# The convolution-gate product in three passes on split operands, in place of plain float32

## The reference, cut to what matters

```
for l in range(2):
    h = rms_norm(x, norm_g[l]) * (1.0 + scale) + shift
    z = h @ w_in[l]
    q_lat, kv_lat, k_rope, mla_gate, conv_in, conv_gate = split(z)
    q, kv = rms_norm(q_lat) @ w_q_up[l], rms_norm(kv_lat) @ w_kv_up[l]
    mla_out = attention(q, k, v) * silu(mla_gate)
    u = u_val * sigmoid(u_gate)                      # from conv_in
    u = causal_depthwise_conv(u, dw_w[l], dw_b[l])   # 31 taps
    u = silu(layer_norm(u)) @ w_pw[l] + b_pw[l]
    conv_out = u * silu(conv_gate)
    x = x + gate * (concat([mla_out, conv_out]) @ w_out[l])
```

## Time and profile before

| | |
|---|---|
| timed runs | 2514.95, 2525.88, 2526.59 us; median 2525.88 |
| the profiled execution | 2515.07 us, its span 2513.3 us |
| TensorE busy (matmuls) | 2300.4 us, 92% |
| VectorE busy | 1775.0 us, 71% |
| ScalarE busy | 909.1 us, 36% |
| `cgate`, layer 0 | from 351.29 us on |
| last mean matmul, layers 0 and 1 | 428.27 and 925.88 us |

### The profile page before, as it was taken

How to read it: one execution, slowest core, us unless ns; L and a number is a source line. 1 busy time by engine, 2 the same in 40 slices (tenths; PEclk the granted TensorE clock), 3 DMA queues, 4 the chain that set the end, 5 groups by cost and what they waited for, 6 DMA issues and landing times.

```text
span 2513.3 us, 41861 instructions
## 1 busy us (share of the span) xinstructions
PE 2300.4 (92%) x16517; PEld 2193.2 (87%) x16517; DVE 1775.0 (71%) x2368; ACT 909.1 (36%) x1330; POOL 48.8 (2%) x61
## 2 busy tenths in 40 slices
PE   2189999999899998998988999988999999999998
PEld 2189998789899977898988998778999999999997
DVE  6777898795778987959768583578866666554443
ACT  1054322324434123244443441135544444443333
POOL 0000000000000000005000000000000000000000
PEclk9698999999889999998999998989999999999999
DMA  8869754787687547967968793346865555556552
GB/s 300 313 227 345 259 169 142 260 304 232 208 303 262 167 158 234 314 222 234 343 217 293 258 333 114 101 151 202 275 210 183 184 182 181 180 169 182 181 182 95
DMA packets 413233, 557.40 MB, mean 222 GB/s; under 512 B 25139, under 2 KB 362103, under 8 KB 412868
## 3 DMA queue, kind: packets, MB, share of 16 engines
q1 hardware_dynamic: 409536, 550.70, 66.9%
q0 software_dynamic: 1120, 2.18, 0.5%
q10 hardware_dynamic: 2468, 3.07, 0.3%
HBM read 553.72 MB, written 2.17 MB: 221 GB/s over the span
## 4 chain that ended last, share of the span: by engine, by line
PE 78%; DVE 12%; DMA 5%; ACT 3%; issue 2%; SPq 0%; DVEq 0%; ACTq 0%
PE gemm L1354 71%; DVE ada_acc L921 4%; DMA ada_raw<-in_ada_w 4%; PE stat L1374 2%; PE stat L1381 1%; DVE w_lo L948 1%; DVE scr L976 1%; DVE h_lo L981 1%; ACT w_hi L675 1%; DMA ada_raw<-in_w_ada 1%; DVE ss L1119 1%; ACT h_full L711 0%; PE bankS L1500 0%; PE bankS L1499 0%; DVE q_tok L1126 0%
## 5 line engine op out<-in xcount | busy, mean ns | idle before, releaser
L948 DVE TENSOR_TENSOR w_lo<-w_raw,w_hi 128x1024 fp32r<-128x1024 f32 (+1 forms) x564 | 671.3, 1201 | 431.6 <-ACT w_hi L675 429.4
L1354 PE MATMUL gemm<-h_hi,w_hi 128*128 128x256 f32 x3136 | 900.5, 287 | 47.4 <-DVE h_lo L981 19.9
L1354 PE MATMUL gemm<-h_lo,w_hi 128*128 128x256 f32 x3136 | 895.9, 286 | 0.0
L1354 PE MATMUL gemm<-h_hi,w_lo 128*128 128x256 f32 x3136 | 895.6, 286 | 0.0
L675 ACT ACTIVATE w_hi<-w_raw 128x1024 fp32r<-128x1024 f32 (+1 forms) x564 | 571.6, 1028 | 740.8 <-PE gemm L1354 590.2
L1354 PEld LDWEIGHTS gemm<-h_hi,w_hi 128*128 128x128 f32 x3136 | 611.6, 195 | 50.7 <-issue 34.6
L1354 PEld LDWEIGHTS gemm<-h_lo,w_hi 128*128 128x128 f32 x3136 | 611.4, 195 | 0.2
L1354 PEld LDWEIGHTS gemm<-h_hi,w_lo 128*128 128x128 f32 x3136 | 610.7, 195 | 0.0
L921 DVE SCALAR_TENSOR_TENSOR ada_acc<-ada_raw,c_act,ada_acc 128x1024 f32<-128x1024 f32 x360 | 460.9, 1297 | 34.7 <-DMA ada_raw<-in_ada_w 28.7
L1354 PE MATMUL gemm<-G_hi,w_hi 128*128 128x256 f32 x704 | 199.3, 283 | 3.1 <-DVE w_lo L948 3.1
L1354 PE MATMUL gemm<-G_lo,w_hi 128*128 128x256 f32 x704 | 199.2, 283 | 0.0
(11 more groups left out here) (269 smaller groups left out, 2562.7 us busy)
## 6 DMA issues: line engine op xcount, KB each, us to landing
w_raw<-in_w_in SPq DMA_DIRECT2D x264, 512.0 KB, 5.5
ada_raw<-in_ada_w SPq DMA_DIRECT2D x192, 512.0 KB, 5.3
w_raw<-in_w_up SPq DMA_DIRECT2D x176, 512.0 KB, 3.5
ada_raw<-in_w_ada SPq DMA_DIRECT2D x168, 512.0 KB, 5.2
w_raw<-in_w_out SPq DMA_DIRECT2D x96, 512.0 KB, 5.4
w_raw<-in_w_down SPq DMA_DIRECT2D x64, 512.0 KB, 3.9
ada_late<-in_w_ada SPq DMA_DIRECT2D x24, 512.0 KB, 4.5
w_raw<-in_w_down SPq DMA_DIRECT2D x32, 384.0 KB, 3.6
```

What stands on the lines that cost most here:

```text
L948: dve.tensor_tensor(w_lo[:, fixed % PARTS, 0:sz], w_raw[:, fixed % RAW, 0:sz], w_hi[:, fixed % PARTS, 0:sz].bitcast(F32), ALU.subtract).th ...
L1354: last = pe.matmul(half(g, k, q), left, right, start=(kt == 0 and j == 0), stop=(u == len(g.units) - 1 and t == nk - 1 and j == len(parts) ...
```

## The change

`cgate` becomes a split product on `h_hi` and `h_lo`, like `gate` before it, and `h_full`, its copies and its semaphore go. The order of the products, the loads and the convolution's steps stay as written.

```diff
-        h_full = at("h_full", W2 + 8, [P, KT, T])
...
-        h_full_ready = sem("h_full_ready")
...
-            G["cgate", l] = product("cgate", wi, 4, CB, full, 4, "a", h_full, None, plain(O_CG))
+            G["cgate", l] = product("cgate", wi, 4, CB, full, 4, "a", h_hi, h_lo, plain(O_CG))
...
-                    if r < LAYERS:
-                        for t in range(KT):
-                            ins = act.activation(h_full[:, t, :], buf[:, t, :], ACT.Identity, bias=mod[:, shift, t:t + 1])
-                        ins.then_inc(h_full_ready, 1)
...
-                pe.wait_ge(h_full_ready, l + 1)
```

## The result

The changed kernel takes 2537.47 us (median of 6 runs, 2534.11 to 2540.95), the kernel before on the same chip 2523.07 us (6 runs, 2514.95 to 2526.59). The ratio is 1.0061, with a 95% interval from 1.0047 to 1.0076: slower by 0.6%, where 1.0% was forecast (2552 us, range 2533 to 2565). Of the profiled executions the one after took 2534.11 us with a span of 2532.3 us, 19.0 us more than the span of before.

What follows compares the result with a forecast made beforehand. TensorE and VectorE were both full where `cgate` stands, TensorE ending last; the change would make VectorE pacemaker. 2 x 14.8 - 6.7 + 2 x 1.5 = +25.9 us on the median 2525.88 gave 2552 us, range 2533 to 2565.

Steps and rivals of the forecast that it cites:

- The case as computed: Whole kernel: VectorE paces `cgate`, start gaps close, some clock is lost; +25.9 us, 2552 us, own range 2541 to 2559, 74%.
- the rival in which half of the lateness is absorbed: VectorE's chain after the last mean: load waits or convolution layout give back some 8 us a layer; 2536 us, 10%.
- The two levels of execution: Timed runs of the kernel before: executions lie at two levels 11 us apart, the profiled one at the lower.
- VectorE becomes the pacemaker, pitch 5.86 us: Beside `cgate`'s units c0 to c15: a split plus 12 convolution operations takes 5.86 us against TensorE's 2.88; 14.8 us later a layer.
- The convolution ends at 441.5, TensorE still arrives last: End of the `cgate` stage: convolution done at 441.5, TensorE at 443.1, so TensorE is last by 1.6 us.
- Clock, +1.5 us a layer: TensorE's clock may fall between waits for splits; loss bounded by 0 and 3 us a layer, 1.5 taken.
- a rival: TensorE's clock stays down through `kv` and `q`, as in `krope`: 6.5 us a layer in place of 1.5, 2562 us, 12%.
- Twelve waits of some 3 us for `w_lo`: TensorE in `cgate`: waits of some 3 us before nearly every unit from c6 on, some 12 a layer.
- The third mean must wait, to 416.0, and is over before c15: In `cgate`: third mean waits for 2 operations behind c14's split, to 416.0, ending before c15, the last of 16 units.
- Both gaps go, -6.7 us: Start of each layer: without `h_full` copies TensorE's idle of 3.04 and 3.69 us goes, -6.7 us for two layers.
- Against which time: Base of the sum: +26 us added to the median before, 2525.88, giving 2552; from the profiled execution, 2541.
- TensorE stays the bound: Rival for the whole kernel: relief of TensorE counts in full, 25 us saved, 2501 us, 4%.

Runs made afterwards that it cites:

- narrow split: Changed kernel with VectorE's subtractions for `cgate` 8 columns wide in place of 1024, leaving out most low parts: 2510.41 us, ratio 0.9958.
- load only: Kernel before, `cgate` plain, with one unused 128x1024 subtraction on VectorE at each of the 16 places of a layer: 2553.90 us, ratio 1.0133.
- the split of one and two blocks: Kernel before with copies moved beside `lat`, plus one or two of four `cgate` blocks split, means unmoved: 2516.13 us (0.9984) and 2527.63 us (1.0032).
- moved copies: Kernel before, `cgate` plain, with the `h_full` copies taken two at a time behind `lat`'s first `w_hi` copies: 2510.00 us (0.9950), again 2507.97 us (0.9957).
- copies kept: Changed kernel with ScalarE's 16 `h_full` copies a layer still made but read by nobody: 2549.15 us, ratio 1.0109.
- the even convolution: Changed kernel with 4 convolution operations beside each `cgate` unit in place of 6, 28 more beside `kv`, means behind units 2, 11, 15: 2537.68 us, ratio 1.0078.

## Why the prediction was right, and where its size was off

The direction and the mechanism of the main term held, and the time lies in the range. That it does is partly luck. The case as computed had a range of its own, 2541 to 2559, and 2537.47 us lies below it, beside the 2536 of the rival in which half of the lateness is absorbed. The mechanism of that rival did not occur: both stages are 15.4 us longer, what stands between them is 1.3 us longer but for the start, and only 3.3 us come back behind the second. What brought the time down is the gain at the second layer's start, which was taken too small, and the scatter of the executions. The two levels of execution that the prediction saw in three runs aren't there either: the six runs of the kernel before lie at 2514.95, 2520.93, 2522.12, 2524.01, 2525.88 and 2526.59 us. By its steps:

- *VectorE becomes the pacemaker, pitch 5.86 us*: 5.89 us. The sum of `lat_kv` was 1.18 us earlier than before in the profiled execution; with that, c15's `w_lo` was forecast at 419.92 - 1.18 = 418.74 and started at 418.77. That VectorE's time is the cause is shown twice, by taking it away (narrow split, stage +2.4 in place of +15.4) and by adding it alone (load only, +17.0 and +15.4).
- *The convolution ends at 441.5, TensorE still arrives last*: 440.58, and the subtraction waited 2.76 us for TensorE, as said.
- *Clock, +1.5 us a layer*: the granted clock went up and down between the waits (0.73 at 376 to 382), was 0.86 at 418 to 424 and 1.00 behind it; it did not stay down through `kv` and `q`. The last mean was forecast at 443.1 - 1.2 = 441.9 without any loss by the clock and began at 442.44: some 0.5 us. (`krope`'s low stretch, which a rival took as a measure, doesn't end with its narrow matmuls: in the first layer of before they start from 182.92 to 197.70, and the low clock of the earlier trace rows lasts from 189 to 202.) This term was 1 us a layer too large, since half the clock was hidden in the pitch as the prediction's 5.0 us for a unit allowed. Stage in all: forecast 14.8 + 1.5 = 16.3, measured 15.4.
- *Twelve waits of some 3 us for `w_lo`*: six, 13.3 us in all, the longest 2.8. The first ones are eaten by TensorE's lead of four buffers, and where the clock is low the unit itself is longer. It changed nothing in the sum.
- *The third mean must wait, to 416.0, and is over before c15*: it began at 415.10, and the chain passes through it. It was one of two conditions that fell within half a microsecond of each other. Behind the mean, c14 ran at low clock until about 419.6, and c15 began at 420.43, 0.4 us after its split would have let it (418.77 + 1.28 = 420.05):

```profile
420.43 0.28 PE L1348 MATMUL gemm<-h_hi,w_hi 128*128 128x256 f32 x1
```

The prediction treated the mean as the one that hides, so the last link of its chain was wrong: in this layer the mean and the clock behind it decided, not c15's split. Load only showed that the mean alone would have given about the same stage. That was no error of size here, but it was what made the expectations for the split of one and two blocks wrong.
- *Both gaps go, -6.7 us*: **this is the step that was mis-sized.** The change of the starts is -2.9 and -8.5 us in the profiled executions, -11.4 together, and in the medians keeping the copies costs 12 us. The first layer was right (3.04 forecast). In the second there was more behind the gap than the gap of 3.69 us. Windows of the kernel before:

```profile
653.00:656.00 3.00, 3.00 (x16) 3.00 (x15) 3.00 (x3) 1.61 (x4) 0.00 (x0) 0.50 0.42 87
680.00:700.00 20.00, 20.00 (x97) 20.00 (x97) 9.94 (x9) 5.73 (x7) 0.00 (x0) 0.51 0.87 282
```

and of the kernel after, where the same work stands 10 us later:

```profile
655.00:691.00 36.00, 36.00 (x304) 36.00 (x303) 31.89 (x38) 16.49 (x26) 0.00 (x0) 1.00 0.78 259
693.00:706.00 13.00, 13.00 (x62) 13.00 (x63) 7.11 (x7) 4.45 (x6) 0.00 (x0) 0.50 0.96 319
```

After the gap of 3.53 us the clock stood at 0.50 for 3 us, in which half the work is lost, some 1.6 us; without the gap it stayed at 1.00 from 655 to 691. The gap of 2.89 us in the first layer had cost no clock, and I took that for both. And the low stretch that begins in `krope`'s narrow matmuls was longer: 20 us before, 13 us after, 7 us at half clock or some 3.4 us. Cut at the starts of matmuls, 5.1 of the 8.5 us lie ahead of `krope` (the gap of 3.7 and the 1.6 behind it make 5.3), 1.9 in its 96 matmuls (started from 677.31 to 694.69 before and from 687.69 to 703.21 after, 17.4 against 15.5 us), and 1.5 between them and the sum of `lat_kv`. That the moved copies bring the whole of it is shown: with them alone the second start is 122.8 us, against 130.9 before. The trace of before had the sign: the clock is at 0.50 behind the gap of 3.53 us of the earlier trace rows, and the prediction priced the gap alone.

- *Against which time*: in the spans the change is +19.0 us, in the medians +14.4. The profiled execution of before was 8 us under its median, that of after 3.4 us under its own. The prediction added its difference to the median of before, so its sum of +25.9 has to be held against 14.4 (another 2.8 us of the distance from 2552 to 2537.47 come from the median before, 2525.88 of three runs and 2523.07 of six). Of these 11.5 us about 5 us are the second layer's start, 2 us the clock in the stage, and the rest, some 5 us, is how the executions of either kernel scatter. The two profiled executions of the version with moved copies show that scatter by themselves, 2505.3 and 2517.9 us of span, and 10 of these 12.6 us lie behind the second stage, where the two programs are the same.

*TensorE stays the bound* (2501 us) did not come true; it would have needed VectorE's time to be free, and even the narrow split reaches only 2510. The Trainium skill's rule (Perfetto Trace Analysis, Identifying the Most-Contended Engine) to optimize the engine of highest occupancy first did not hold for this change: TensorE is highest by matmuls, 92%, and by the weight loads that the section names for it, 87%; the change took work from it, and the time rose, since both engines were full where the product stands.

Open: whether the longer low stretch in `krope` comes from the gap 25 us ahead of it. The three kernels that make the copies in one piece (before, copies kept, load only) take 17.2 to 17.4 us for `krope`'s 96 matmuls in the second layer, the ten executions without the gap 15.2 to 15.9. But the even convolution, which has no gap, took 17.6 us in its first layer, so there is a second cause, and the share of the gap isn't settled.

## What to carry to other kernels

Where two engines are both full, count what an edit adds to the one in the same unit as what it takes from the other: here 1.14 us on VectorE for 0.57 us on TensorE, 18.2 us a layer against a slack of 6.6, and the one other spread of the convolution that was tried gave back 1.6 us. Slack read at the end of a stage (6.55 us at the last mean) is not there for work in its middle while the other engine's queue holds an earlier wait for it; find the first such wait, and move it before you spend the slack. And look at what a change takes along: the gain was in the copies that the new product made needless, and they could be moved without it.

## What the runs showed of the hardware

- A VectorE operation with two inputs in SBUF and a GpSimd subtraction did not overlap: one such operation beside each subtraction took 2.6 us in place of 0.40, and 18 took 22.23 us in place of 7.21. Two operations with one input, at 388.07, took 4.80 us together in place of 0.74. Behind a close row of VectorE's operations one GpSimd subtraction, 2.47 us otherwise, was shown at 18.80 us.
- A gap of TensorE of 2.89 us was followed by a granted clock of 1.00, one of 3.53 us by 0.50; with the copies kept, 3.47 us of idle in the second layer gave the lower one again (0.52 in the window above). The length alone doesn't decide: in the changed kernel's stage, with several waits close behind one another, none over 2.85 us, the clock was 0.73 from 376 to 382.
- These waits left the granted clock at 0.91 over the stage. The last of them ended at 415.10, and the clock was at 1.00 only from about 419.6 on.
- At half clock a matmul took 0.21 us in `krope` (64 columns) as in the split product (256 columns).
- A unit of the split product took 2.88 us for 24 matmuls, against 3.45 us for the plain one, which is 17% less. By the Trainium skill (FP8 and Floating Point Precision, TensorE Precision Notes) true float32 is four passes. By an estimate from that page three in place of four would be 25% less, which these rows do not bear out.
